# An S5 recurrence at every fourth time step in a two-layer fp32 transformer kernel

## The chip, the cores and the metric

One core of a Trainium2 chip runs the whole program. The metric is the device time of one execution in microseconds (us), lower being better.

## The reference

A stack of two layers over 512 positions of width 1024, batch 1, all in fp32. Each layer is an FFN (SwiGLU, hidden width 2816), a mixer, cross attention over 256 memory rows, and a second FFN; RMS norms stand before each. The mixer of layer 0 is the one that is changed: it projects the normed stream into the inputs of a chunked gated linear attention (GLA) and into `u`, 512 channels for S5. S5 has 32 groups of 16 channels with 64 complex states each:

```python
mag = exp(min(lam_re, -1e-4) * dt);  ab = mag * exp(i * lam_im * dt)     # one complex number per state
bb = f * B                                       # f = (ab - 1) / lambda
x[t] = ab * x[t-1] + bb @ u[t]                   # the recurrence, 512 time steps
y[t] = Re(C) @ Re(x[t]) - Im(C) @ Im(x[t]) + D * u[t]
y = gelu(y);  y = y * sigmoid(y @ w_glu + b_glu)
```

32 groups of 64 states make 2048 states, or 16 state tiles of 128 partitions (two groups each). `y` is joined to the GLA output and projected back. The mixer of layer 1 is a sparse attention and plays no part here.

## The kernel before, in words

**Weights.** All weight matrices are one stream of 381 blocks of 128x1024. SyncE loads them by halves into two raw slots (L236 to L266). GpSimd splits each half (L271 to L285) into a high and a low part, with a wait for TensorE to have finished the same half of the block two earlier, then three instructions: a 128x1 gate (L279), a rounding copy (L280) and a subtraction (L284). So GpSimd is at most two blocks ahead of TensorE. TensorE multiplies with three fp32r matmuls for one product (`mm3`, L310 to L312); one block gives 24 of them with 512 columns (a `tile`, L327), or with 256 columns for the keys and values of the memory (`kv_tile`, L452).

**Order.** Every engine has its own program, written out by hand, and semaphores join them: FFN 0, norm 1, then the even mixer. In it four tiles of `u` are projected (L340, `project`), then nine more tiles (the low-rank input of the decay, and q, k, r of the GLA), four blocks of GLA values (`values`, L487), the two alpha matmuls (L513), five blocks of memory keys (blocks 83 to 87), the two blocks of the S5 gate (`glu`, L624), and the GLA itself (`gla`, L522), whose first lines put three more memory key blocks ahead of its transposes (L525, L530). VectorE evicts each projected tile with `tile_out` (L1399).

**S5 before.** The recurrence is made real by rotating the states: with tables of cos and sin of the state's angle at each time, VectorE turns the input backwards, runs a real scan with factor `mag`, and turns the result forwards. The 16 tables of 128x1024 (cos, sin) are made during FFN 0: VectorE reduces the angle (`turns`, L1492, six instructions for each table), ScalarE takes the sines (`table`, L889) and writes the table to DRAM (L905); L1060 loads it again. At the end of FFN 0 VectorE multiplies C by f (`s5_output_matrices`, L1587, seven instructions). The loop of `s5` then goes over 16 state tiles, one at a time: TensorE makes the input (`inputs`, L592: K = 32 channels, 512 columns, one matmul for the real and one for the imaginary part), VectorE does four products from PSUM (L1638 to L1643), two sums, two scans of 512 steps (L1650, L1652), four products and two sums (L1655 to L1665), and TensorE multiplies by C (`outputs`, L605: 32 output channels, K = 128). Between them TensorE runs one weight block for each state tile (`ev_fill`, L773), in a fixed order: block, `inputs(j + 1)`, `outputs(j)`.

An fp32 matmul stands as two records in the trace, so that 32 calls of L602 give 64 records; an fp32 transpose is one record.

The lines that the text names, besides those: L324 is the mean square of a norm, L1309 its reciprocal, L1371 the low part of a hidden tile for the down projection (`part`), which TensorE needs before it takes that block, L1595 to L1602 the weight products, L1622 the sum with D * u, L1266 the low part of `y` that `glu` waits for, L1075 the gelu, L1088 the eviction of the values, L518 alpha, L1471 and L1472 two of the 16-column constants of S5, L741 transposes of the cross attention, L557 scores of the GLA, and L664 the logits of layer 1's indexer, whose calls go to partitions 0 to 63 and 64 to 127 in turn (L661).

## Time and profile before

| | us |
|---|---|
| median of 3 runs | 2435.99 |
| lowest, highest | 2433.85, 2439.0 |
| span of the profiled execution | 2432.6 |
| TensorE busy in it | 2301.4 |
| VectorE busy in it | 1154.7 |
| GpSimd busy in it | 1738.1 |

The profiled execution's span counts from its first to its last instruction. PE is TensorE's matmuls, PEld its weight loads, DVE VectorE, ACT ScalarE, POOL GpSimd. Durations of neighbours overlap a little, so the cost of one instruction in a row of them is read from the distance between starts. PEclk is the granted TensorE clock, 1.0 being 2.4 GHz and 0.5 being 1.2 GHz.

### The profile page before, as it was taken

The page shows a single profiled execution, that of the slowest core. Times are in us where ns is not written, and L with a number is a line of the kernel's source. Part 1 is how long each engine was busy: PE and PEld are TensorE (multiplying, and loading weights), DVE is VectorE, ACT ScalarE, POOL GpSimd, SP SyncE. Part 2 cuts the span into 40 slices and gives each one's busy share as a digit, 9 for nine tenths or more (in the row PEclk, how much of TensorE's full clock was granted, in tenths as well). Part 3 has the DMA queues.
Part 4 walks back from the last instruction along what each step waited for, and adds up shares of the span by engine and source line. Part 5 has one row for each costly group of instructions (what it writes and reads, how often), then busy time and mean ns, then how long its engine had stood idle before and what let it go on. Part 6 is the DMA issues. An engine that isn't in the chain of part 4 may idle for free.

```text
span 2432.6 us, 31471 instructions
## 1 busy us (share of the span) xinstructions
PE 2301.4 (95%) x10068; PEld 1820.2 (75%) x10068; DVE 1154.7 (47%) x1468; ACT 435.1 (18%) x752; POOL 1738.1 (71%) x2287
## 2 busy tenths in 40 slices
PE   7999999888789999999999999999987999999997
PEld 6888786445678688888778888877765777888886
DVE  7577717998644342224244223144598333322314
ACT  2122212002221221111122101120134222111011
POOL 7788877565648377878787788876764746777874
PEclk9999999897889999999999999999999999999998
DMA  4244334222212123333232323332221212323332
GB/s 158 90 144 146 126 95 134 78 91 78 70 57 95 49 83 95 98 96 100 91 108 87 99 95 95 100 94 83 78 74 53 81 58 77 96 95 97 96 96 82
DMA packets 117312, 226.02 MB, mean 93 GB/s; under 512 B 13040, under 2 KB 13312, under 8 KB 116864
## 3 DMA queue, kind: packets, MB, share of 16 engines
q1 hardware_dynamic: 110736, 203.61, 26.5%
q10 hardware_dynamic: 6512, 21.52, 2.6%
q8 instruction: 45, 0.74, 0.1%
q14 instruction: 19, 0.16, 0.0%
HBM read 214.59 MB, written 10.49 MB: 93 GB/s over the span
## 4 chain that ended last, share of the span: by engine, by line
PE 79%; DVE 15%; issue 2%; ACT 2%; POOL 1%; DMA 0%; SPq 0%; ACTq 0%; DVEq 0%; POOLq 0%
PE ps L310 24%; PE ps L311 24%; PE ps L312 24%; DVE tg L1286 1%; DVE arena L1738 1%; PE ps L728 1%; DVE col L1737 1%; PE ps L753 1%; DVE x L1276 1%; DVE sg L1652 1%; PE ps L602 1%; DVE sg L1650 1%; PE ps L643 1%; PE ps L613 1%; DVE arena L1757 0%
## 5 line engine op out<-in xcount | busy, mean ns | idle before, releaser
L310 PE MATMUL ps<-x,w_split 128*128 128x512 f32 (+1 forms) x2872 | 1126.3, 392 | 39.6 <-POOL w_split L284 17.4
L311 PE MATMUL ps<-x,w_split 128*128 128x512 f32 (+1 forms) x2872 | 1110.3, 387 | 0.0
L312 PE MATMUL ps<-x,w_split 128*128 128x512 f32 (+1 forms) x2872 | 1110.0, 386 | 0.0
L284 POOL TENSOR_TENSOR w_split<-w_raw,w_split 128x512 fp32r<-128x512 f32 x762 | 1021.5, 1341 | 63.5
L279 POOL TENSOR_TENSOR gate<-gate 128x1 f32<-128x1 f32 x758 | 257.7, 340 | 602.2 <-PE ps L312 601.9
L310 PEld LDWEIGHTS ps<-x,w_split 128*128 128x128 f32 x2872 | 544.4, 190 | 180.6 <-POOL w_split L284 28.0
L311 PEld LDWEIGHTS ps<-x,w_split 128*128 128x128 f32 x2872 | 544.5, 190 | 110.1 <-issue 4.8
L312 PEld LDWEIGHTS ps<-x,w_split 128*128 128x128 f32 x2872 | 543.9, 189 | 108.8
L280 POOL TENSOR_SCALAR w_split<-w_raw 128x512 fp32r<-128x512 f32 x762 | 509.4, 669 | 4.5 <-DMA w_raw<-in_stream 4.5
L1371 DVE TENSOR_TENSOR x<-arena,x 128x512 fp32r<-128x512 f32 x88 | 87.3, 1008 | 284.6 <-ACT x L941 284.6
L1328 DVE TENSOR_TENSOR tu<-ps,rstd 128x512 f32<-128x512 f32 x88 | 60.7, 689 | 319.5 <-PE ps L312 319.5
L887 ACT ACTIVATE sg<-tg 128x512 f32<-128x512 f32 x88 | 55.6, 632 | 652.1 <-DVE tg L1325 646.9
L1325 DVE TENSOR_TENSOR tg<-ps,rstd 128x512 f32<-128x512 f32 x88 | 60.6, 689 | 192.1 <-PE ps L312 191.3
L1334 DVE TENSOR_TENSOR arena<-sg,tu 128x512 f32 (+1 forms) x88 | 107.6, 1222 | 27.3 <-ACT sg L887 17.8
L1301 DVE SCALAR_TENSOR_TENSOR h<-ps,h 128x512 f32<-128x512 f32 x64 | 44.0, 688 | 142.9 <-PE ps L312 142.4
L941 ACT ACTIVATE x<-arena 128x512 fp32r (+1 forms) x88 | 53.7, 628 | 313.1 <-PE ps L312 312.4
L849 ACT ACTIVATE x<-h,vec 128x512 fp32r<-128x512 f32 x64 | 46.2, 722 | 210.7 <-DVE h L1301 206.9
L1399 DVE TENSOR_TENSOR arena<-ps,rstd 128x512 f32<-128x512 f32 x45 | 30.7, 689 | 101.4 <-PE ps L312 100.9
L1276 DVE SCALAR_TENSOR_TENSOR x<-h,vec,x 128x512 fp32r<-128x512 f32 x64 | 67.9, 1060 | 7.9 <-ACT x L849 7.9
L1286 DVE TENSOR_TENSOR tg<-tg,sq 128x512 f32<-128x512 f32 x63 | 70.0, 1110 | 0.1
L310 PE MATMUL ps<-w_split,x 128*128 128x256 f32 (+1 forms) x192 | 66.4, 346 | 1.3 <-POOL w_split L284 1.2
L311 PE MATMUL ps<-w_split,x 128*128 128x256 f32 (+1 forms) x192 | 61.1, 318 | 0.0
(234 smaller groups left out, 1576.5 us busy)
## 6 DMA issues: line engine op xcount, KB each, us to landing
w_raw<-in_stream SPq DMA_DIRECT2D x762, 256.0 KB, 2.6
s_tables<-kv ACTq DMA_DIRECT2D x16, 512.0 KB, 3.4
arena<-s_tables ACTq DMA_DIRECT2D x16, 512.0 KB, 3.3
out<-h ACTq DMA_DIRECT2D x8, 256.0 KB, 2.2
h<-in_xT SPq DMA_DIRECT2D x1, 1536.0 KB, 8.7
arena<-in_memT SPq DMA_DIRECT2D x1, 1024.0 KB, 10.5
arena<-in_memT ACTq DMA_DIRECT2D x1, 1024.0 KB, 4.8
h<-in_xT SPq DMA_DIRECT2D x1, 512.0 KB, 3.9
```

Source lines behind the costliest of these rows:

```text
L279: pool.tensor_tensor(gate[:, 0:1], gate[:, 1:2], gate[:, 1:2], ALU.add)
L280: pool.tensor_scalar(W[:, s, 0, c], raw[:, s, c], 1.0, 0.0, ALU.mult, ALU.add).then_inc(S(f"w_hi{'ab'[half]}"), 1)
L284: pool.tensor_tensor(W[:, s, 1, c], raw[:, s, c], W[:, s, 0, c].bitcast(F32), ALU.subtract).then_inc(split_ready if half else S("half_spli ...
L310: pe.matmul(dst, wh, xh, start=start, stop=False)
L311: pe.matmul(dst, wh, xl, start=False, stop=False)
L312: return pe.matmul(dst, wl, xh, start=False, stop=stop)
L1276: dve.scalar_tensor_tensor(X[to][:, k, 1, :], h[:, k, :], gain(n, k), X[to][:, k, 0, :].bitcast(F32), ALU.mult, ALU.subtract).then_inc(S(" ...
L1286: ins = dve.tensor_tensor(tg[:, 0, :], tg[:, 0, :], sq[:, k % 2, :], ALU.add)
L1325: dve.tensor_tensor(tg[:, s, :], ps[:, BANKS[2 * s], :], rstd[:], ALU.mult).then_inc(S("gate_ready"), 1)
L1328: dve.tensor_tensor(tu[:, s, :], ps[:, BANKS[2 * s + 1], :], rstd[:], ALU.mult).then_inc(S("up_ready"), 1)
L1334: dve.tensor_tensor(dst, sg[:, s:s + 1, :], tu[:, s:s + 1, :], ALU.mult).then_inc(S("hid_done"), 1)
L1371: dve.tensor_tensor(X[xo][:, ch:ch + 1, 1, :], hid[:, d, :], X[xo][:, ch:ch + 1, 0, :].bitcast(F32), ALU.subtract).then_inc(S("x_lo"), 1)
```

## The change

The recurrence is run for every fourth time step only. `u` is stored by offset within four steps (`by_offset`): four stretches of 128 columns. The input of step k of the strided recurrence is the sum over the four offsets of `ab^(3-s) * B` times `u`, so that `inputs` accumulates four matmuls of 128 columns; the tables and the scans have 128 steps, and one VectorE operand holds four state tiles side by side. The output at offset 3 is C times the state; at offsets 0 to 2 it is C times `ab^1` to `ab^3` times the state of the step before, plus a direct product of `u` with short taps (`C * f * ab^m * B`, block-diagonal, three 128x128 matrices for each of four channel tiles). 16 tables become 4. The powers of `ab` (32 more 16-column instructions), four sets of output weights and three sets of input weights are computed on VectorE, the latter between the parts of FFN 0's down projection; the input weights are turned by 24 transposes on TensorE beside the first `u` tiles, with copies by ScalarE, and the taps are 24 fp32 matmuls of 128x128x128, masked by VectorE. The order of TensorE's work in the stage is written out anew (`even_inputs`), and `y` goes to the other operand buffer. The masks of the taps, the eviction banks (`EV_BANKS` = 2, 3, 0 in turn) and the bank of the outputs (1) are new. `s5_input_weights` is like `s5_output_weights`, for powers of `ab` times B. The diff, cut to its core:

```diff
+STRIDE = 4
+NK = T // STRIDE
...
+                if beside is not None:
+                    beside(0)
                 mean_square(n)
                 for t in (2, 3):
                     tile(at + t, ((at + t) % 2, BANKS[t]), x)
+                    if beside is not None:
+                        beside(t - 1)
...
+            def s5_weights(i):
+                pe.wait_ge(S("h_ready"), 8)
+                pe.wait_ge(S("s5_mul"), 14)
+                if i == 0:
+                    pe.wait_ge(S("mat_in"), 16)
+                else:
+                    pe.wait_ge(S("s5_w"), 2 * i)
+                for c in range(2):
+                    for q in range(4):
+                        m = pe.transpose(ps[:, 6 + c, q * P:(q + 1) * P], b_in(i, c)[:, q * P:(q + 1) * P], ident)
+            def s5_taps(i):
+                if i == 0:
+                    pe.wait_ge(S("b_raw"), 16)
+                if i == 1:
+                    pe.wait_ge(S("std_ready"), 2)
+                if i == 2:
+                    pe.wait_ge(S("s5_tau"), 1)
+                for q in range(4):
+                    qc = slice(q * P, (q + 1) * P)
                     for c in range(2):
+                        m = pe.matmul(ps[:, TAP_BANKS[i], qc], area(A_BRAW + c * T)[:, qc], c_out(i, c)[:, qc],
+                                      start=(c == 0), stop=(c == 1))
+                m.then_inc(S("s5_tap_mm"), 1)
+            def s5_beside(step):
+                s5_weights(step)
+                if step == 2:
+                    s5_taps(0)
+            def s5_inputs(q):
+                pe.wait_ge(S("proj_out"), 4)
+                if q == 0:
+                    pe.wait_ge(S("s5b_in"), 16)
+                    pe.wait_ge(S("s5_tau"), 3)
+                    pe.wait_ge(S("rcol_ready"), 1)
+                    pe.wait_ge(S("s5_w"), 6)
+                else:
+                    pe.wait_ge(S("s5_read"), q)
+                for c in range(2):
+                    for s in range(STRIDE):
+                        for jj in range(4):
+                            r = slice(32 * jj, 32 * jj + 32)
+                            m = pe.matmul(ps[:, IN_BANKS[jj], c * NK:(c + 1) * NK], b_in(s, c)[r, q * P:(q + 1) * P],
+                                          Pt[q][r, s * NK:(s + 1) * NK], start=(s == 0), stop=(s == STRIDE - 1))
+                m.then_inc(S("s5_in_mm"), 1)
+            def s5_outputs(q):
+                pe.wait_ge(*((S("s5_y"), q) if q else (S("s5_tau"), 3)))
+                for i in range(3):
+                    pe.matmul(ps[:, OUT_BANK, i * NK:3 * NK], taps[:, i, q, :], Pt[q][:, 0:(3 - i) * NK],
+                              start=(i == 0), stop=False, skip_group_check=True)
+                pe.wait_ge(S("s5_x"), 2 * q + 2)
+                for r in (3, 0, 1, 2):
+                    for c in range(2):
+                        for jj in range(4):
+                            x = sq[:, c, jj * NK:(jj + 1) * NK]
+                            at = r * NK
+                            w = c_out((r + 1) % 4, c)[:, (4 * q + jj) * 32:(4 * q + jj + 1) * 32]
+                            out_r = ps[32 * jj:32 * jj + 32, OUT_BANK, :]
+                            if r == 3:
+                                m = pe.matmul(out_r[:, at:at + NK], w, x, start=False, stop=False,
+                                              skip_group_check=True)
+                            else:
+                                m = pe.matmul(out_r[:, at + 1:at + NK], w, x[:, 0:NK - 1], start=False,
+                                              stop=(r == 2 and c == 1), skip_group_check=True)
+                m.then_inc(S("s5_out_mm"), 1)
...
+                free = 1 if t == 4 else t - 2
+                tile(EV_AT + t, ((EV_AT + t) % 2, EV_BANKS[(t - 4) % 3]), 1, (S("proj_out"), free))
...
+                ev_tile(4)
+                s5_taps(1)
+                s5_taps(2)
+                rstd_columns(0)
+                ev_tile(5)
+                s5_inputs(0)
+                ev_tile(6)
+                s5_inputs(1)
+                ev_tile(7)
+                ev_tile(8)
+                s5_outputs(0)
+                ev_tile(9)
+                s5_inputs(2)
+                ev_tile(10)
+                s5_outputs(1)
+                ev_tile(11)
+                ev_tile(12)
+                s5_inputs(3)
+                s5_outputs(2)
+                pe.wait_ge(S("proj_out"), 13)
+                pe.wait_ge(S("s5_read"), 4)
+                values(EV_V_AT, 0, T, EV_V_BANKS)
+                values(EV_V_AT, 1, T, EV_V_BANKS)
+                s5_outputs(3)
+                values(EV_V_AT, 2, T, EV_V_BANKS)
+                values(EV_V_AT, 3, T, EV_V_BANKS)
+                gla_alpha()
+                for t in range(EARLY_KEYS):
+                    kv_tile(0, t, KV_BANKS)
...
+                    [(S("h_ready"), 3)], [(S("h_ready"), 8)], beside=s5_beside)
+            even_inputs()
...
+                    act.dma_start(area(A_CRAW, 2 * T), s5c.rearrange("p c j o -> p (c j o)")).then_inc(S("s5c_in"), 16)
+                    act.dma_start(area(A_BRAW, 2 * T), s5bt.rearrange("p c j o -> p (c j o)")).then_inc(S("b_raw"), 16)
+                    for i in range(last):
+                        if 4 <= i < 8:
+                            table(i - 4)
...
+            def s5_load(q):
+                act.dma_start(area(A_ROT + (q % 2) * 2 * T, 2 * T), s5_tables[q]).then_inc(S(f"s5_tab{q % 2}"), 16)
...
+                    act.wait_ge(S(f"tab_out{s}"), 32)
+                act.wait_ge(S("x_lo"), X_LO_HID[0] + FC)
+                act.dma_start(area(A_BIN[3], 2 * T), s5b.rearrange("p c q s -> p (c q s)")).then_inc(S("s5b_in"), 16)
+                act.dma_start(block_mask, blocks).then_inc(S("blocks_in"), 16)
+                for q in range(2):
+                    s5_load(q)
+            def s5_weights():
+                for i in range(3):
+                    act.wait_ge(S("s5_tr"), i + 1)
+                    for c in range(2):
+                        act.activation(b_in(i, c), ps[:, 6 + c, :], ACT.Copy).then_inc(S("s5_w"), 1)
...
+                act.wait_ge(S("s5_in_mm"), 4)
+                act.dma_start(chunk_mask, rows[1:2, :].to_broadcast([P, T])).then_inc(S("cmask_in"), 16)
+                act.dma_start(wal, w_alpha).then_inc(S("wal_in"), 16)
+                s5_gelu(2)
...
+                act.wait_ge(S("s5_out_mm"), 4)
+                act.wait_ge(S("block_done"), EV_V_AT + 4)
+                act.wait_ge(S("rcol_ready"), 1)
+                for tt in range(4):
+                    act.activation(val[:, tt, :], ps[:, EV_V_BANKS[tt], :], ACT.Copy,
+                                   scale=col[:, 16 + tt:17 + tt]).then_inc(S("gla_v"), 1)
+                gla_log()
...
+                        if i < 4:
                             next(parts)
+                        elif i < 8:
+                            turns(i - 4)
...
-                if f == 0:
-                    for s in range(2):
-                        turns(last, s)
+                    for d in range(4, 20):
+                        part(slice(d, d + 1), d % 4, base + d + 1)
+                        if 5 <= d < 9:
+                            s5_output_weights(d - 5)
+                        elif 9 <= d < 12:
+                            s5_input_weights(d - 9)
...
+            def ev_out(t):
+                if t < 4:
+                    dve.tensor_tensor(by_offset(Pt[t]), ps[:, BANKS[t], :].rearrange("p (k s) -> p k s", s=STRIDE),
+                                      rstd[:].rearrange("p (k s) -> p k s", s=STRIDE), ALU.mult
+                                      ).then_inc(S("proj_out"), 1)
...
                 chain(dve.tensor_tensor(fi, fi, den, ALU.mult))
                 yield
...
+                times(L_POW + 2, L_POW, L_POW)
+                times(L_POW + 4, L_POW + 2, L_POW)
+                for m in range(1, STRIDE):
+                    times(G_POW + 2 * m, G_POW, L_POW + 2 * (m - 1))
...
-                    ph, pl = sc5[:, C_PH + j:C_PH + j + 1], sc5[:, C_PL + j:C_PL + j + 1]
+                time = area(A_TIME).rearrange("p (j k) -> p j k", j=4)
+                ph = sc5[:, C_PH + 4 * q:C_PH + 4 * q + 4].unsqueeze(2).to_broadcast([P, 4, NK])
...
+                chain(dve.tensor_tensor(a, time, ph, ALU.mult))
+                chain(dve.tensor_scalar(b, a, MAGIC, MAGIC, ALU.add, ALU.subtract))
+                chain(dve.tensor_tensor(a, a, b, ALU.subtract))
+                chain(dve.tensor_tensor(b, time, pl, ALU.mult))
+                chain(dve.tensor_tensor(a, a, b, ALU.add))
+                chain(dve.tensor_scalar(b, a, MAGIC, MAGIC, ALU.add, ALU.subtract))
+                dve.tensor_tensor(a, a, b, ALU.subtract).then_inc(S("s5_turn"), 1)
...
+            def s5_output_weights(m):
...
+                dve.tensor_tensor(er, cr, gr, ALU.mult)
+                chain(dve.tensor_tensor(tA, ci, gi, ALU.mult))
+                dve.tensor_tensor(ei, cr, gi, ALU.mult)
+                chain(dve.tensor_tensor(tB, ci, gr, ALU.mult))
+                dve.tensor_tensor(er, er, tA, ALU.subtract).then_inc(S("s5_mul"), 1)
+                dve.scalar_tensor_tensor(ei, ei, -1.0, tB, ALU.mult, ALU.subtract).then_inc(S("s5_mul"), 1)
...
+            def s5_input_weights(i):
...
+            def s5_tap(i):
+                dve.tensor_tensor(taps[:, i], ps[:, TAP_BANKS[i], :].rearrange("p (q n) -> p q n", q=4),
+                                  block_mask.unsqueeze(1).to_broadcast([P, 4, P]), ALU.mult).then_inc(S("s5_tau"), 1)
...
+                for q in range(4):
...
+                    dve.wait_ge(S(f"s5_tab{q % 2}"), 16 * (q // 2 + 1))
+                    dve.wait_ge(S("s5_in_mm"), q + 1)
+                    if q >= 1:
+                        dve.wait_ge(S("s5_x"), 2 * q)
+                    op(dve.tensor_tensor(four(p1), vr, four(c), ALU.mult))
+                    n2 = op(dve.tensor_tensor(four(p2), vi, four(s), ALU.mult))
+                    op(dve.tensor_tensor(four(p3), vi, four(c), ALU.mult))
+                    dve.tensor_tensor(four(p4), vr, four(s), ALU.mult).then_inc(S("s5_read"), 1)
...
+                    ev_out(5 + 2 * q)
+                    for z, p, n in ((zr, p1, nr), (zi, p3, ni)):
+                        after(n)
+                        for jj in range(4):
+                            k = slice(jj * NK, (jj + 1) * NK)
+                            mag = sc5[:, C_MAG + 4 * q + jj:C_MAG + 4 * q + jj + 1].to_broadcast([P, NK])
+                            n = op(dve.tensor_tensor_scan(z[:, k], mag, p[:, k], 0.0, ALU.mult, ALU.add))
+                    ev_out(6 + 2 * q)
+                    after(n)
...
+                    if q >= 1:
+                        dve.wait_ge(S("s5_out_mm"), q)
                     after(n2)
+                    dve.tensor_tensor(xr, p1, p2, ALU.subtract).then_inc(S("s5_x"), 1)
                     after(n4)
-                    dve.tensor_tensor(xi, p3, p4, ALU.add).then_inc(S("s5_xi"), 1)
-                    if j % 4 == 0 and j >= 4:
-                        out(j // 4 - 1)
+                    dve.tensor_tensor(xi, p3, p4, ALU.add).then_inc(S("s5_x"), 1)
+                    if q >= 1:
+                        out(q - 1)
+                    if q >= 2:
+                        lower(q - 2)
+                out(3)
+                lower(2)
+                lower(3)
...
+                    x = X[0][:, 4 + n, :, :].rearrange("p c (k s) -> p c k s", s=STRIDE)
+                    lo_of(x[:, 1], by_offset(Pt[n]), x[:, 0], X_LO_GLU + n + 1)
...
+                ev_out(t)
+            dve.wait_ge(S("blocks_in"), 16)
+            s5_tap(0)
+            s5_tap(1)
+            s5_tap(2)
             rstd_columns(0)
+            ev_out(4)
+            s5()
```

## Rows read from the trace of the kernel before

**Rows 1.** the profile page: engine busy times, then 40 slices in tenths.

```profile
PE 2301.4 (95%) x10068; PEld 1820.2 (75%) x10068; DVE 1154.7 (47%) x1468; ACT 435.1 (18%) x752; POOL 1738.1 (71%) x2287
...
PEclk9999999897889999999999999999999999999998
```

**Rows 2.** busy time by stretch; the first line names the columns.

```profile
core 0: us, PE busy (x) PEld busy (x) DVE busy (x) ACT busy (x) POOL busy (x), PEclk, DMA share, GB/s
64.00:266.00 202.00, 201.73 (x880) 164.54 (x880) 144.53 (x176) 46.19 (x71) 167.93 (x213) 1.00 0.40 128
...
416.00:620.00 204.00, 171.32 (x570) 96.18 (x569) 191.71 (x242) 17.11 (x25) 120.02 (x109) 0.87 0.26 81
620.00:647.00 27.00, 21.02 (x112) 19.05 (x113) 18.44 (x20) 12.51 (x18) 22.71 (x27) 0.87 0.26 79
1325.00:1565.00 240.00, 240.00 (x1061) 198.87 (x1060) 65.23 (x74) 30.70 (x46) 192.00 (x265) 1.00 0.31 97
```

**Rows 3.** timeline of VectorE over one state tile, 428 to 440 us (start, duration).

```profile
428.04 0.68 DVE L1638 TENSOR_TENSOR tg<-ps,arena 128x512 f32<-128x512 f32 x1
...
431.63 1.22 DVE L1650 TENSOR_TENSOR_SCAN sg<-sc,tg 128x512 f32<-128x512 f32 x1
432.76 1.20 DVE L1652 TENSOR_TENSOR_SCAN sg<-sc,tu 128x512 f32<-128x512 f32 x1
...
439.22 0.69 DVE L1638 TENSOR_TENSOR tg<-ps,arena 128x512 f32<-128x512 f32 x1 [1.06 <-issue]
```

**Rows 4.** VectorE by line in 416:616 (count, busy us, mean ns, idle before).

```profile
L1652 DVE TENSOR_TENSOR_SCAN sg<-sc,tu 128x512 f32<-128x512 f32 x16 | 24.7, 1545 | 0.0
...
L1658 DVE TENSOR_TENSOR tu<-sg,arena 128x512 f32<-128x512 f32 x16 | 16.7, 1042 | 0.0
```

**Rows 5.** chain of waits, 612 to 648 us (start, us, what).

```profile
613.86 3.41 DVE x L1266 x3
...
620.04 0.50 PE ps L310
...
628.01 1.85 POOL w_split L284
...
647.03 1.07 PE ps L530 x5
```

**Rows 6.** input and output matmuls by source line (ns min, median, max).

```profile
L602 PE MATMUL ps<-arena,kv x64: 587/588/692, 414.5 to 596.8; 32*128 32x512 f32 x64
...
L613 PE MATMUL ps<-arena,kv x32: 592/617/1062, 427.7 to 614.3; 128*32 128x512 f32 x32
```

**Rows 7.** constants of S5 on VectorE in 86:93.

```profile
L1471 DVE TENSOR_TENSOR tiny<-tiny 128x16 f32<-128x16 f32 x1 | 1.1, 1146 | 0.0
...
L1472 DVE TENSOR_TENSOR tiny<-vec 128x16 f32<-128x16 f32 x1 | 0.2, 176 | 0.0
```

**Rows 8.** end of the first FFN: weight products on VectorE, a TensorE wait.

```profile
288.65 0.50 PE L310 MATMUL ps<-x,w_split 128*128 128x512 f32 x1 [0.97 <-DVE x L1371]
...
369.18 0.70 DVE L1595 TENSOR_TENSOR tu<-kv,sc 128x512 f32<-128x512 f32 x1 [1.85 <-DMA kv<-in_s5c]
...
375.27 1.39 DVE L1602 TENSOR_SCALAR kv<-kv 128x512 f32<-128x512 f32 x1
```

**Rows 9.** VectorE, the eviction of the fourth projected tile.

```profile
413.59 0.69 DVE L1399 TENSOR_TENSOR arena<-ps,rstd 128x512 f32<-128x512 f32 x1 [4.76 <-PE ps L312]
```

**Rows 10.** short fp32 matmuls and transposes on TensorE, three timelines.

```profile
1747.11 1.13 PE L664 MATMUL ps<-arena 64*128 64x256 f32 x8 [1.48 <-DVE arena L1875]
...
670.13 1.05 PE L557 MATMUL ps<-arena 64*128 64x128 f32 x8
...
826.04 1.07 PE L741 MATMUL ps<-mat,arena 128*128 128x128 f32 x8 [2.81 <-DVE arena L1818]
```

**Rows 11.** value copies and alpha matmuls, by source line (ns).

```profile
L1088 ACT ACTIVATE arena<-ps,col x4: 670/682/694, 574.2 to 576.0; 128x512 f32<-128x512 f32 x4
...
L518 PE MATMUL ps<-arena,kv x4: 1056/1057/1187, 576.8 to 579.5; 16*128 16x512 f32 x4
```

More of the change, by code:

```diff
@@ L133 @@
 NV = 141
-C_MAG, C_PH, C_PL, C_FR, C_FI = [16 * i for i in range(5)]
+C_MAG, C_PH, C_PL = [16 * i for i in range(3)]
+L_POW, G_POW = 0, 6
 A_TIME = FC * T
@@ L161, with build_trunk @@
 A_XPT = A_XP + 4 * T
-def build_trunk(nc, xT, memT, pos, vecs, w_alpha, s5b, s5c, mats, mask, rows, stream, out):
+def build_trunk(nc, xT, memT, pos, vecs, w_alpha, s5b, s5bt, s5c, blocks, mats, mask, rows, stream, out):
     with ExitStack() as ctx:
@@ L822, in _ @@
             for q in range(2):
[L823 removed]
+                values(OD_V_AT, q, 2 * P, BANKS)
             indexer_weights()
@@ L914, in ffn @@
                             s5_constants()
-                        if i == 3:
-                            for s in range(2):
-                                table(i, s)
-                    with act.Fori(4, last) as i:
-                        for s in range(2):
-                            silu(i, s)
-                        for s in range(2):
-                            table(i, s)
+                        if 4 <= i < 8:
+                            table(i - 4)
                 elif f == 2:
@@ L948, in ffn @@
                     silu(last, s)
-                if f == 0:
-                    for s in range(2):
-                        table(last, s)
                 act.wait_ge(S("hid_done"), FC * (f + 1))
@@ L1339, in ffn @@
                     parts = s5_constants()
-                    for i in range(4):
+                    for i in range(last):
                         for s in range(2):
@@ L1344, in ffn @@
                             memory(0)
-                        if i < 3:
+                        if i < 4:
                             next(parts)
-                        else:
-                            for s in range(2):
-                                turns(i, s)
-                    with dve.Fori(4, last) as i:
-                        for s in range(2):
-                            gate(i, s)
-                        for s in range(2):
-                            turns(i, s)
+                        elif i < 8:
+                            turns(i - 4)
                 elif f == 2:
@@ L1381, in ffn @@
                     gate(last, s)
-                if f == 0:
-                    for s in range(2):
-                        turns(last, s)
                 dve.wait_ge(S("hid_done"), FC * (f + 1))
@@ L1387, in ffn @@
                     beside()
-                with dve.Fori(1, 5) as i:
-                    for s in range(4):
-                        part(bass.ds(i * 4 + s, 1), s, i * 4 + (base + s + 1))
+                if f == 0:
+                    for d in range(4, 20):
[4 more added lines that the diff above has]
+                            s5_input_weights(d - 9)
+                else:
+                    with dve.Fori(1, 5) as i:
+                        for s in range(4):
+                            part(bass.ds(i * 4 + s, 1), s, i * 4 + (base + s + 1))
                 for d in (20, 21):
@@ new lines, in turns, with by_group, power @@
+                chain(dve.tensor_tensor(a, a, b, ALU.subtract))
[3 more added lines that the diff above has]
+                dve.tensor_tensor(a, a, b, ALU.subtract).then_inc(S("s5_turn"), 1)
+            def by_group(x):
+                return x.rearrange("p (j o) -> p j o", j=16)
+            def power(at):
+                return (powers[:, at + c, :].unsqueeze(2).to_broadcast([P, 16, 32]) for c in range(2))
@@ L1974, in lay_out @@
     s5b = np.zeros((P, 2, 4, P), f)
-    s5c = np.zeros((P, 2, S5_TILES, 32), f)
+    s5c, s5bt = (np.zeros((P, 2, S5_TILES, 32), f) for _ in range(2))
     for g in range(32):
```

321 lines of the change are left out of this document (126 added, 195 removed).

## The prediction

> **What bounds the kernel now.** First the page: TensorE is busy for 2301.4 of 2432.6 us, and its clock is full in nearly every slice [rows 1]. So the general answer is "TensorE", and a change to VectorE's work should be worth nothing. The table by stretch says where that is wrong. In an FFN (1325 to 1565) TensorE is busy without a break, 1061 records in 240.0 us, and 24 of them, one weight block, take 5.43 us. In the S5 stretch, 416 to 620, it is VectorE that is full: 191.7 of 204 us, with TensorE at 171.3 and at a mean clock of 0.87 [rows 2].
>
> One state tile on VectorE shows why. The four products from PSUM start 0.60 us apart, the two scans 1.13 us apart, and the next tile's first product comes 11.2 us after this one's [rows 3]. That is the quiet case; with GpSimd working beside it a product of two SBUF operands has a mean of 1.04 us and the second scan 1.55 us, not 0.60 and 1.13 [rows 4]. 16 tiles from 416 to 613.9 us [rows 5] are 12.3 us each. TensorE has less to do for a tile: a block (5.43), an input pair and an output pair, 1.7 us each at full clock (four records of 512 columns at 0.11 us for each 128 [rows 10]). It waits for VectorE, loses its clock, and then costs VectorE something in turn.
>
> What follows is the second half of the story. `glu` waits for the last low part of `y` until 620.0, and from there the chain runs through GpSimd's splits to the GLA transposes at 647.0 [rows 5]. GpSimd needs six instructions for a block: from the busy times and counts that is 4.35 us in the FFN, 4.73 where VectorE is busy for 72% of the time, 5.05 in 620 to 647, and 6.61 in the S5 stretch [rows 2]. A memory key block costs TensorE only about 2.8 us (24 matmuls of 256 columns), so a run of them goes at GpSimd's pace.
>
> **The change, part by part.** I count on the old clock from 413.5, where the fourth `u` tile is done (evicted at 413.6 [rows 9]), to the transposes of L530 at 647.0: 233.5 us.
>
> *Tables and powers.* 16 tables of six VectorE instructions become four of seven. TensorE runs 64 to 266 us without a break (201.7 of 202.0 [rows 2]), so this is worth nothing: what hides it is the weight stream. The 32 new 16-column instructions cost between 0.18 and 1.15 us each [rows 7]; with the durations seen that is some 10 us in one turn of the loop, where the turns before took longer in the same place. Nothing. The last two tables stood ahead of the down projection, and TensorE waited 0.97 us for a hidden tile there [rows 8]: -1.0. The two 512 KB loads at the start have 100 us to land, and the s5b and table loads, now behind VectorE's last hidden part, have 45 us.
>
> *Weights between the down parts.* Seven sets of six instructions. The old set of seven ran from 369.2 to 376.7, 1.07 us each [rows 8], so one set takes 6.4 us and, with the part, VectorE needs 7.3 us for a block of 5.43. A part is ready three blocks ahead of its use, 16 us; seven sets eat 13 us of that. VectorE should just get through. GpSimd is the doubt: beside a full VectorE it takes up to 6.6 us a block against TensorE's 5.43, over eight blocks 0 to +9 us. I take +3.0, nearer to the stretch with VectorE at 72%.
>
> *Transposes and first taps.* Eight transposes take 1.07 us [rows 10], of which the last record's tail overlaps: 3 x 1.0. Eight matmuls 128x128x128: four calls of 128 columns stand as 8 records in 1.05 us [rows 10], tail included, so 0.22 a call: 1.8. TensorE goes on with block 4 at 413.5 + 4.8 = 418.3. The six copies by ScalarE run behind the next `u` tile each time.
>
> *Inputs.* For each group 32 calls of 128 columns with K = 32, in four different groups of 32 rows in turn. Alone they are 32 x 0.22 = 7.0 us (before: eight calls of 512, 6.9). But the trace has calls that do not run alone: the indexer's go to rows 0 to 63 and 64 to 127 in turn, and eight records of 256 columns take 1.13 us [rows 10], the time of eight with 128. So two run at once. Four at once would be 1.75 us. I take two, 3.5 us, the nearest row.
>
> *Outputs.* Three tap matmuls, 768 columns: 1.3 us. 32 calls with 32 output columns, four column groups in turn: no row shows such calls together, L613 has one group at a time [rows 6]. Between 7.0 and 1.75; I take 3.5, as for the rows: 4.8 us.
>
> *VectorE.* A group of four tiles is now 16 instructions of 512 columns (12 of the recurrence, two evictions, the sum with D * u, a low part) and 8 scans of 128 (a quarter of 1.13 us and a fixed part, some 0.33 each): 12 us quiet, 16 with the durations of [rows 4]. TensorE has 28 us of work for a group. From `inputs(q)` to the finished state are 11 to 14 us, and TensorE has 19.8, over 25, 24.6 and 15.7 us of other work before it needs it. One wait stays: `values` needs the 13th eviction, which stands behind the scans of the last group, 7.5 to 9.5 us after `inputs(3)`, while TensorE arrives after `outputs(2)`, 4.8 us: 3.0.
>
> *The sum.* From 418.3: nine blocks 48.9, taps and the rstd transposes 4.0, inputs 4 x 3.5 = 14.0, outputs 4 x 4.8 = 19.2, values 21.7, the wait 3.0, together 110.8: the values are done at 529.1. Alpha waits for four copies of 0.68 [rows 11], 2.7, and takes 1.7 at full clock: 533.5. From the middle of the first key block (+1.4) eight more blocks come at GpSimd's pace: 4.9 us, between 4.35 and 5.05 [rows 2], as VectorE does the decay meanwhile: 39.2, and a last half, 1.4. The transposes start at 575.5: 71.5 us earlier. ScalarE's gates are done some 10 us before. With -1.0 and +3.0 in the FFN, 69.5. The strided evictions, and the eight strided splits of `y` ahead of the output projection, have no row; between nothing and twice 0.6 us they are 0 to +5, and I take 0, as they have the length of [rows 3]. 2432.6 - 69.5 = 2363.1 is the span; the median stands 3.4 above the profiled span, so 2366.5.
>
> A rule of the Trainium skill speaks against the change: TensorEngine Tiling (Array Packing), section Tiling Modes, says that a change of the tiling mode drains the array. With a record's tail of 0.16 us for each of 16 changes the time would be 2369; no run here shows it yet.
>
> **The rivals.**
> *A, four at once.* Inputs 1.75 and outputs 3.05 us. For it: the indexer's pairs overlap fully, so the row groups do not disturb each other [rows 10]. Against it: no row shows more than two, or any column groups. 4 x 3.5 less: 2352.5. The same skill page, section Theoretical Speedup, gives up to four times for a dimension of 32 or less.
> *B, one after the other.* A fixed cost for each weight load and matmul sets the pace: nowhere in [rows 10] do records come more than one each 0.11 us on average, whatever their columns. Then 7.0 and 8.3 us: +28, 2394.5.
> *C, GpSimd late in the down projection.* VectorE's products against its splits, at the S5 stretch's 6.6 us [rows 2]: +9 in place of +3, and some more where the parts come late: 2376.
> *D, slower.* The groups do not only fail to overlap, they break the pipeline: each record of 128 columns pays its share and its whole tail, 0.11 + 0.16 = 0.27 us (a 588 ns record of L602 [rows 6] less 0.43). 64 records are 17.3 us, 4 x 27.6 = 110 more: 2477. It decides from 0.19 us a record on (69.5 us over 512 records above the 0.055 assumed). The indexer's row is against it for the inputs; nothing is for the outputs, which alone would give 2422.
>
> That the change doesn't do what it says I leave out: loops, tables and instruction counts are in the diff.
>
> **How the numbers follow.** Forecast 0.45, A 0.20, B 0.20, C 0.10, D 0.05. The forecast's own range, with GpSimd at 4.35 to 5.5 us and the FFN at 0 to 9, is 2358 to 2378. A with the low bounds reaches 2345, B with the high ones 2403. I give 2343 to 2402, which leaves out D and the outer ends of A and B. A measurement of this kernel tells 0.2%, 4.9 us, from no change. All cases but D are faster by far more; of D I put 0.01 into no change.
>
> **What the profile would show.** VectorE's busy share in the S5 stretch falls from 0.94 to about a half; TensorE has no wait for VectorE but one near 3 us ahead of the values; `inputs` spans 3.5 us and `outputs` 4.8; the transposes of L530 start near 577 us (575.5 and the 2 of the FFN); the clock stays at 2.4 GHz from 416 to the values. I would be wrong if `inputs` took 7 us or more, if TensorE waited for GpSimd in the down projection for more than 9 us, or if waits for VectorE filled the time that the scans gave free.

## The result, and the profile after

The changed kernel takes 2365.68 us (median of 4 runs, 2365.23 to 2368.07) against 2437.38 for the kernel before on the same chip: ratio 0.972, 95% interval 0.9699 to 0.9741. The profiled span fell from 2432.6 to 2363.4 us. I had 2366.5.

In the changed kernel L338 to L340 are the three matmuls of a product, L670 is the input call, L678 the tap matmuls, L689 and L692 the output calls, L646 the taps, L550 alpha and L562 the GLA transposes, all on TensorE. On VectorE L1448 makes the low part of a hidden tile, L1642 to L1663 are the weight products, L1486 evicts a projected tile, L1779 to L1805 are the recurrence. On ScalarE L1179 copies the values and L1073 evicts a key tile. On GpSimd L307 is the gate, L308 the rounding copy and L312 the subtraction.

The page, to be laid beside [rows 1]:

```profile
span 2363.4 us, 31958 instructions
...
PE 2251.5 (95%) x10548; PEld 1827.9 (77%) x10548; DVE 1024.3 (43%) x1327; ACT 416.4 (18%) x721; POOL 1707.6 (72%) x2287
...
PEclk9999999998899999999999999999999999999998
```

Busy times by stretch, in the columns of [rows 2]. First the down projection with the weight products; then 416 to the last value matmul; then from there to the GLA transposes:

```profile
284.00:336.00 52.00, 45.46 (x194) 35.71 (x193) 51.59 (x43) 5.05 (x8) 49.32 (x51) 1.00 0.27 86
416.00:523.00 107.00, 102.15 (x911) 84.42 (x909) 58.92 (x102) 7.43 (x11) 59.57 (x82) 0.98 0.24 78
523.00:581.00 58.00, 45.47 (x248) 39.81 (x248) 20.21 (x20) 22.82 (x34) 46.59 (x58) 0.85 0.28 89
```

The S5 stretch is TensorE's now: it is busy for 102.2 of 107 us, at a clock of 0.98; VectorE went from 191.7 of 204 us [rows 2] to 58.9 of 107, a share of 0.55. The stretch behind it is GpSimd's. The down projection is where VectorE is full, 51.6 of 52 us. What TensorE waited for, first in the down projection, then from 410 to 590:

```profile
PE ps L338 <- POOL w_split L312: 3.9, 4, 1.2
PE ps L338 <- DVE x L1448: 2.6, 2, 1.6
...
PE ps L338 <- POOL w_split L312: 10.5, 7, 3.4
PE ps L338 <- DVE arena L1486: 4.2, 1, 4.2
PE ps L550 <- ACT arena L1179: 2.7, 1, 2.7
```

The first input step and the first output step on TensorE:

```profile
433.79 0.39 PE L340 MATMUL ps<-x,w_split 128*128 128x512 f32 x1
434.11 2.07 PE L670 MATMUL ps<-arena 32*128 32x128 f32 x64
436.11 0.50 PE L338 MATMUL ps<-x,w_split 128*128 128x512 f32 x1
436.44 0.40 PE L339 MATMUL ps<-x,w_split 128*128 128x512 f32 x1
...
455.71 1.46 PE L678 MATMUL ps<-arena 128*128 128x384 f32 x6
457.10 0.65 PE L689 MATMUL ps<-sq,kv 128*32 128x128 f32 x16
457.56 1.48 PE L692 MATMUL ps<-sq,kv 128*32 128x127 f32 x48
458.97 0.50 PE L338 MATMUL ps<-x,w_split 128*128 128x512 f32 x1
```

An input step is 2.0 us from its start to the next block's, not the 3.5 I took; an output step 3.3, not 4.8. The starts of single records in the trace come four within 20 ns and then 91 ns later: four groups at once, 112 ns for a record of each.

A change of the shape has a price too. The block's first record starts 0.20 us after the last record of an input or output step. Behind the taps, which use the whole array, it starts 0.03 us after the last of them:

```profile
417.27 1.95 PE L646 MATMUL ps<-kv,arena 128*128 128x128 f32 x16
418.98 0.48 PE L338 MATMUL ps<-x,w_split 128*128 128x512 f32 x1
419.30 0.40 PE L339 MATMUL ps<-x,w_split 128*128 128x512 f32 x1
```

From the last short record to the block's second it is 0.54 us in the one case and 0.35 in the other, so a change costs 0.19 us; ahead of an input step it is again 0.19, ahead of an output step's short calls 0.12. About half of this lies inside the 2.0 and 3.3 us. (The 0.3 us between the block's first two records are no sign of it: they stand behind the taps as well.)

VectorE's part of a group, beside [rows 3]:

```profile
436.31 0.69 DVE L1779 TENSOR_TENSOR tg<-ps,arena 128x512 f32<-128x512 f32 x1 [6.54 <-PE ps L670]
...
440.52 2.41 DVE L1793 TENSOR_TENSOR_SCAN sg<-sc,tg 128x128 f32<-128x128 f32 x4
442.85 1.34 DVE L1793 TENSOR_TENSOR_SCAN sg<-sc,tu 128x128 f32<-128x128 f32 x4
444.11 0.66 DVE L1486 TENSOR_TENSOR arena<-ps,rstd 128x512 f32<-128x512 f32 x1
...
447.70 0.68 DVE L1805 TENSOR_TENSOR sq<-tu 128x512 f32<-128x512 f32 x1
```

12.1 us for four state tiles (with two evictions), where one took 11.2. The first group has no sum with D * u yet; the others take 15.3, 12.7 and 11.7 us with it; the 15.3 are the group that ran longest beside GpSimd's splits.

### The profile page after: what moved, and what is told of

Same layout as the page of the kernel before. It is cut to its first block, busy times and chain, and to the rows that moved or that the text cites. A ratio compares the mean times of both kernels' runs of the same rounds, so it can differ in the third digit from the quotient of the medians.

```text
span 2363.4 us, 31958 instructions
## 1 busy us (share of the span) xinstructions
PE 2251.5 (95%) x10548; PEld 1827.9 (77%) x10548; DVE 1024.3 (43%) x1327; ACT 416.4 (18%) x721; POOL 1707.6 (72%) x2287
## 4 chain that ended last, share of the span: by engine, by line
PE 77%; DVE 12%; issue 5%; POOL 4%; ACT 1%; DMA 0%; POOLq 0%; SPq 0%; DVEq 0%; ACTq 0%
PE ps L338 24%; PE ps L340 24%; PE ps L339 24%; POOL w_split L312 2%; POOL w_split L308 2%; DVE tg L1369 2%; PE ps L800 1%; DVE arena L1879 1%; DVE col L1878 1%; PE ps L825 1%; DVE x L1359 1%; POOL gate L307 1%; DVE arena L1898 0%; DVE col L1901 0%; DMA h<-in_xT 0%
## 5 line engine op out<-in xcount | busy, mean ns | idle before, releaser
L338 PE MATMUL ps<-x,w_split 128*128 128x512 f32 (+1 forms) x2872 | 1125.5, 392 | 43.8 <-POOL w_split L312 25.3
L340 PE MATMUL ps<-x,w_split 128*128 128x512 f32 (+1 forms) x2872 | 1110.0, 386 | 0.0
L312 POOL TENSOR_TENSOR w_split<-w_raw,w_split 128x512 fp32r<-128x512 f32 x762 | 1015.8, 1333 | 63.6
L338 PEld LDWEIGHTS ps<-x,w_split 128*128 128x128 f32 x2872 | 545.0, 190 | 171.5 <-POOL w_split L312 31.7
L307 POOL TENSOR_TENSOR gate<-gate 128x1 f32<-128x1 f32 x758 | 243.5, 321 | 563.8 <-PE ps L340 561.0
L340 PEld LDWEIGHTS ps<-x,w_split 128*128 128x128 f32 x2872 | 544.7, 190 | 108.5
L308 POOL TENSOR_SCALAR w_split<-w_raw 128x512 fp32r<-128x512 f32 x762 | 500.2, 656 | 4.3 <-DMA w_raw<-in_stream 4.3
L1448 DVE TENSOR_TENSOR x<-arena,x 128x512 fp32r<-128x512 f32 x88 | 87.7, 1013 | 246.0 <-ACT x L1028 246.0
L338 PE MATMUL ps<-w_split,x 128*128 128x256 f32 (+1 forms) x192 | 65.5, 341 | 5.1 <-DVE arena L1486 4.2
L1492 DVE TENSOR_TENSOR arena<-ps,rstd 128x512 f32<-128x512 f32 x32 | 21.9, 691 | 96.5 <-PE ps L340 96.2
```

Of the source, the lines that this page charges most:

```text
L307: pool.tensor_tensor(gate[:, 0:1], gate[:, 1:2], gate[:, 1:2], ALU.add)
L308: pool.tensor_scalar(W[:, s, 0, c], raw[:, s, c], 1.0, 0.0, ALU.mult, ALU.add).then_inc(S(f"w_hi{'ab'[half]}"), 1)
L312: pool.tensor_tensor(W[:, s, 1, c], raw[:, s, c], W[:, s, 0, c].bitcast(F32), ALU.subtract).then_inc(split_ready if half else S("half_spli ...
L338: pe.matmul(dst, wh, xh, start=start, stop=False)
L340: return pe.matmul(dst, wl, xh, start=False, stop=stop)
L1448: dve.tensor_tensor(X[xo][:, ch:ch + 1, 1, :], hid[:, d, :], X[xo][:, ch:ch + 1, 0, :].bitcast(F32), ALU.subtract).then_inc(S("x_lo"), 1)
```

## The experiments

### Do the calls overlap because their groups come in turn?

Three kernels that change nothing but the order of the calls: e1 and e2 in the input step, e3 in the output step.

```
e1   for c in range(2):
-        for s in range(STRIDE):
-            for jj in range(4):
+        for jj in range(4):
+            for s in range(STRIDE):
e2   for c in range(2):
-        for s in range(STRIDE):
-            for jj in range(4):
+        for s, jj in [(s, 2 * h + j) for h in range(2) for s in range(STRIDE) for j in range(2)]:
e3 - for r in (3, 0, 1, 2):
-        for c in range(2):
-            for jj in range(4):
+    for jj in range(4):
+        for r in (3, 0, 1, 2):
+            for c in range(2):
```

> The changed kernel with the 32 calls of an input step in another order: all four time steps of one group of 32 rows, then the next group. Same calls, same number, same data. In the changed kernel 64 records of an input step take 2.07 us, 31 ns each. Theory T (the groups run at once because they come in turn): now each record waits for the one before, 0.11 us as the short calls in the kernel before, 7.0 us a step, 4 x 5.0 = 20 us more, 2385.7 us. Rival S (a call with K = 32 costs 31 ns whatever the order): 2.07 us a step, 2365.7 us.

> The changed kernel with the calls of an input step ordered so that two row groups come in turn, then the other two. Theory T: two at once, 0.055 us a record, 3.5 us a step (the price that the prediction took), 4 x 1.45 = 6 us more, 2371.5 us. If the floor of 31 ns is the issue of a record and two groups are enough to reach it: 2.1 us, 2365.7 us. Rival S: 2365.7 us too.

> The changed kernel with the 32 calls of an output step ordered by column group: all eight calls of one group of 32 output columns, then the next. In the changed kernel the 64 records take 1.9 us. Theory T: 0.11 us a record, 7.0 us a step, 4 x 5.1 = 20.5 us more, 2386 us. Rival S (32 columns make a call short whatever the order): 2365.7 us.

The first input step of e2:

```profile
434.82 2.84 PE L670 MATMUL ps<-arena 32*128 32x128 f32 x64
```

and of e1:

```profile
435.29 5.13 PE L670 MATMUL ps<-arena 32*128 32x128 f32 x64
```

The same 64 records take 2.07 us with four groups in turn, 2.84 with two, 5.13 with one. Rival S is out: shortness alone is not it. T is right in kind and too high in size, since where the order moves on to the next group, its first three records still start beside the last ones of the old group (2 to 7 ns apart in the starts), so even the serial order is not 7.0. Two in turn give 2.84 for the same reason and not 3.5. In time: e1 2381.08 us (ratio to before 0.976, 0.9743 to 0.9777), 15.4 above the changed kernel's median, where the four steps add 11.9 (the other three take 5.03 each). Part of the rest is the clock: in e1's trace TensorE, though busy without a break, fell to 1.2 GHz for 3.4 us at 440.1 and at 477.6 us, at the end of the first and the third serial step, which it did in no other version of the changed kernel between 416 and 490 us; e2 2368.11 (0.9721, 0.9702 to 0.974), where they add 3.1: not to be told from the changed kernel.

e3 took 2376.86 us (0.9743, 0.9724 to 0.9762). Its output calls run from 458.39 to 464.3 us, 5.9 in place of 1.9, so 16 us in all, and yet the kernel is only 11 slower. The wait in front of the values shows most of why: there TensorE had 4.2 us to spare, and the longer `outputs(2)` fills it. Nor does the clock fall there (see the section on the hardware), which is worth another 1.5.

```profile
PE ps L338 <- DVE arena L1486: 0.2, 1, 0.2
```

### How much of the gain is VectorE's?

b1 is the kernel before with the recurrence left out for three quarters of its columns:

```
-  op(dve.tensor_tensor(p1, vr, c, ALU.mult))
+  op(dve.tensor_tensor(p1[:, 0:128], vr[:, 0:128], c[:, 0:128], ALU.mult))
   (the other nine products and sums, and both scans, likewise; not xr and xi)
```

> The kernel before with VectorE's recurrence cut to a quarter: products from PSUM, sums, scans and back-rotations work on the first 128 of 512 columns, so the recurrence is left out for the rest; TensorE's calls and everything else stay. Theory V (VectorE's time in the S5 stretch is what the change took away): VectorE needs some 5.5 us a tile, TensorE 5.4 + 3.5 = 8.9; 13 tiles end near 532, five key blocks at GpSimd's pace, glu and the key blocks behind it: L530 near 592 to 597 in place of 647, so 50 to 55 us less, 2382 to 2387 us. Rival W (the shorter input and output calls are most of the gain, 16 x 3.4 us of TensorE's time become 21 us): not more than 20 us less, 2417 us or above.

2379.19 us, ratio 0.9758 (0.9742 to 0.9774), span 54.9 below that of before. Its busy times from 416 on and its chain where the GLA transposes begin (L530):

```profile
416.00:530.00 114.00, 114.00 (x389) 65.91 (x388) 60.89 (x186) 2.55 (x3) 50.85 (x74) 1.00 0.36 113
...
594.84 0.89 PE ps L530 x8
```

TensorE is full for 114 of 114 us at full clock, and the transposes start 52 us earlier than at 647.0 [rows 5]. Theory V holds: cutting VectorE's time alone gives 54.9 of the 69.2 us. The 14.3 left I put down to TensorE, from the traces; the other half of the test, the short calls with VectorE's time left as it was, was not run. In b1 a block with its input and output calls takes 9.4 us, so about 3.8 us of calls in each of the 13 tiles up to the end of the values, 49 us (those of the last three tiles lie beside GpSimd's splits). The changed kernel has 21 us of them, but 8 us of new transposes and taps and the wait of 4.2, and it comes into the stage 2.0 us later and loses 1.5 to the clock. That makes 12.3 us; its values end at 523.2 us, b1's at 535.1.

### Are the waits that are left worth their time?

```
e4 (down projection)
-  if 5 <= d < 9:
-      s5_output_weights(d - 5)
-  elif 9 <= d < 12:
-      s5_input_weights(d - 9)
+  if 5 <= d < 19:
+      next(weights)          # three of a set's six instructions
e5 (TensorE, behind the values; KV_BANKS = [5, 3])
+  kv_tile(0, 0, KV_BANKS)
   gla_alpha()
-  for t in range(EARLY_KEYS):
+  for t in range(1, EARLY_KEYS):
e6 (VectorE, last group)
+  if q == 3: ev_out(11); ev_out(12)     # ahead of the products
-  ev_out(5 + 2 * q)   ...   ev_out(6 + 2 * q)
+  if q < 3: ev_out(5 + 2 * q)   ...   if q < 3: ev_out(6 + 2 * q)
e7   the three together
```

> The changed kernel with the seven sets of weight products cut in halves of three instructions, one half behind each of 14 down parts in place of one set behind each of 7. In the changed kernel TensorE waits 6.5 us there: 3.9 for GpSimd's splits, whose block takes 6.0 us beside a VectorE that is full, and 2.6 for late parts, as a set takes 9.0 us. Theory P (both waits come from doing the sets faster than the parts are used): VectorE keeps pace (about 5.2 us a part), GpSimd falls behind by at most 0.2 us a block; waits of 0 to 3 us, 3.5 to 6.5 us less, 2359 to 2362 us. Rival Q (the contention for VectorE's and GpSimd's operands costs what it costs, spread or not): the waits show again over 14 parts, 2365.7 us.

> The changed kernel with the first memory key block ahead of the two alpha matmuls, and its PSUM bank exchanged with the second's so that it needs none of ScalarE's value copies. In the changed kernel GpSimd stands still for 8.1 us (523.6 to 531.8) with both weight buffers full, while TensorE waits 2.7 us for the copies and takes 2.9 for alpha. Theory G (GpSimd's pace sets the stretch from the values to the GLA transposes, so its idle time there is worth itself): it resumes 5.6 us earlier, all behind it comes 4.5 to 5.6 us earlier, 2360 to 2361 us. Rival K (the decay for the GLA, which stays where it is, or the key tiles' evictions by ScalarE end last): within 1 us of 2365.7.

> The changed kernel with the 12th and 13th evictions ahead of the last group's products on VectorE, in place of ahead of and behind its scans. In the changed kernel TensorE waits 4.2 us for the 13th before the values. Theory E: the wait falls to the read of the last input bank, 0.7 us; 3.5 us less, 2362.2 us. Rival F (the stretch behind is paced by GpSimd, and an earlier start of the values is lost in it): 2365.7 us.

> The changed kernel with the three edits together: half sets, the key block ahead of alpha, the evictions first. If the three are independent, as theories P, G and E have it: 5 + 5 + 3.5 = 13.5 us less, 2352 us. If they overlap (one wait taking the place of another), less than 9 us less, above 2357 us.

Medians 2361.38, 2362.97, 2363.84 and 2356.43 us; ratios to before 0.9708, 0.9715, 0.9717 and 0.9682 (0.9657 to 0.9707). They ran on another chip, where the kernel before takes 2430.86 us, so the ratios are the fair comparison. By them e4 to e6 gain 2.9, 1.2 and 0.7 us and e7 9.3, between its two expectations. The first three are each within the interval of 0.972, so for them the traces must speak.

e4: TensorE's waits in the down projection, 6.5 us before, are

```profile
PE ps L338 <- DVE x L1359: 2.2, 3, 1.3
PE ps L338 <- POOL w_split L312: 2.1, 7, 0.4
```

of which the first line is the norm behind the down projection, in every kernel. No wait for a part is left, and 4.1 us are won there (start of GpSimd's 41st and 141st split, each against the changed kernel's). Theory P.

e5: GpSimd resumes at 525.2 us, not 531.8, but then stands still again:

```profile
525.21 0.19 POOL L307 TENSOR_TENSOR gate<-gate 128x1 f32<-128x1 f32 x1 [1.15 <-PE ps L340]
...
537.91 0.73 POOL L307 TENSOR_TENSOR gate<-gate 128x1 f32<-128x1 f32 x1 [4.30 <-PE ps L340]
```

TensorE waits 3.4 us ahead of the third key block for ScalarE, which evicts the first key tile only behind the decay's log steps. The GLA transposes start at 577.0 us, 3.7 earlier: theory G, with part of its gain turned into the new wait. How much of it reaches the end, the 1.2 us by the ratio can't tell.

e6: the wait of 4.2 us for L1486 is not among the waits of its trace, and the splits behind the values come 3.2 us earlier, the transposes 2.9, both counted from the S5 stage's start: theory E. Its profiled run was longer than the changed kernel's all the same, by what the clock did elsewhere (below).

e7 joins the three. Against the changed kernel its transposes start at 566.37 in place of 580.68, 14.3 us earlier, and its end comes 7.9 us earlier. To separate this from scatter, it ran again beside the changed kernel, together with e8, which adds one move on ScalarE:

```
e8 (ScalarE, behind the value copies)
+  fill(0, KV_BANKS, 1)
   gla_log()
   ...
-  fill(0, KV_BANKS, EARLY_KEYS)
+  fill(0, KV_BANKS, EARLY_KEYS - 1)
```

> The changed kernel once more, unaltered, beside the two versions below on the same chip: 2365.7 us, within 0.2% (2361 to 2370).

> The version with the three edits again, now beside the changed kernel. Its transposes for the GLA started 14.3 us earlier than in the changed kernel's trace, its end came 7.9 us earlier. If the 14.3 are the edits' and the rest is the clock in the stages behind, which differs from one execution to the next: 7 to 14 us below the changed kernel of the same call, 2352 to 2359 us. If the edits bring nothing beyond the scatter of chips and calls: within 4 us of the changed kernel.

> The version with the three edits, and on ScalarE the eviction of the first key tile ahead of the three log steps of the decay. In the version before it TensorE waits 3.4 us for that eviction ahead of the third key block, and GpSimd stands still for 3.8 us at the same time. Theory G (GpSimd's idle time in this stretch is worth itself): 3.4 to 3.8 us less than the version with the three edits. Rival K (the decay, delayed by the eviction, or a later wait takes it back): the same, within 1 us.

The changed kernel: 2364.89 us, ratio 0.9718 (0.9692 to 0.9744). The three edits: 2353.81, 0.967 (0.9644 to 0.9696), 11.1 us or 0.5% better. The intervals of the two ratios just touch, but the slowest of its five runs, 2357.14, is below the fastest of the changed kernel's five, 2363.6. e8: 2352.05, 0.9662 (0.9637 to 0.9687); its wait for the eviction is gone,

```profile
PE ps L338 <- POOL w_split L312: 8.5, 5, 2.6
PE ps L338 <- ACT kv L1073: 0.5, 1, 0.5
```

but of the 3.4 to 3.8 us only a part shows: 2.7 in the trace at the transposes (counted from the S5 stage's start, against the second run of the three edits; 2.2 against the first) and 1.8 in the median. That is more than rival K allows and less than theory G has. It is the fastest of all, though not to be told from the three edits alone.

## Why the prediction was right, and where it was only lucky

**The mechanism held.** VectorE bounded the S5 stretch, and b1 shows that taking its time away is worth 54.9 us. A group takes it 11.7 to 15.3 us (12 to 16 said), its share is 0.55 (about a half), the one wait ahead of the values is 4.2 us (3.0). The clock stayed at 2.4 GHz from 416 to 495.9 us, the end of that wait; it fell there, just ahead of the values.

**The time is right to a microsecond by errors that cancel.** On the new clock, with the 2 us that I gave to the FFN:
- *Input and output steps.* "I take two, the nearest row" is the term that was mis-sized: four run at once, in rows and in columns, as rival A had it. The eight steps cost 21 us in place of 33. The indexer's row only showed two because its calls have only two groups. The Trainium skill, TensorEngine Tiling (Array Packing), section Theoretical Speedup, gives up to four times for a dimension of 32; by e1 and e3 the gain over the serial order is 2.5 times for rows (5.13 to 2.07 us) and 3 for columns (5.9 to 1.9); that order still overlaps a little, and against 64 records at 0.11 us, 7.0, it would be 3.4 and 3.6. Its rule that a change of the tiling mode drains the array (Tiling Modes) agrees with the 0.20 us between the last record of a step and the block behind it, against 0.03 behind the taps. At 0.12 to 0.19 us the 16 changes come to some 2.8 us, half of it in the steps' own time; I had priced it at 2.5, and left it out of the sum.
- *The values* ended at 523.2, not 531.1 (529.1 and 2): 12.1 us less in the steps and 1.3 at the start of the stretch, against 1.2 more of waiting for the eviction, 0.6 for a split, 1.6 in the blocks beside other calls (5.54 to 5.68 us in place of 5.43), and 1.5 that the values lost in a spell of 3.4 us at 1.2 GHz from 495.9 us. Had the rest held, the result would have been 2358.6, over halfway to rival A's 2352.5.
- *The stretch behind the values* took that back: 57.5 us to the transposes in place of 46.4. I had counted eight blocks after the first; the trace has nine (18 half splits, 531.8 to 579.1 us). GpSimd splits by pairs of blocks, the first halves of both and then the second halves, so one half of the second block was still to do and one of the eleventh stood ahead of the last that was needed. That is a miscount, 5.1 us. GpSimd's pace was 5.1 us a block, not 4.9 (1.5 us), it stood still for 1.7 us more with both buffers full beside `glu`, the first key block held its buffer for 3.1 us and not 1.4, and copies and alpha took 5.5 and not 4.4.
- *The FFN.* The old last tables cost more than the 0.97 us that I took: GpSimd's 101st split starts at 289.9 us, 3.9 earlier than before. (1.7 of the 3.9 are there by the 41st, and there the traces of the changed kernel and its variants differ among themselves by up to 2.3, so that part may be scatter.) Then the weight products take 5.9 back (its 121st split starts 2.0 later), not 3.0; this is rival C's mechanism at two thirds of its price, with a part of its own that I excluded: "VectorE should just get through". One set takes 9.0 us with its part, not 7.3, so the parts themselves came late, 2.6 us of the 6.5.
- *The GLA* gave 3.6 us: its transposes are 66.1 us earlier, what follows it 69.7. The change does nothing there, so this is luck: b1, which has the old GLA, keeps its distance to the changed kernel within 0.2 us over this stage, and a second trace of the changed kernel (c1) gains another 2.9 us in it.

So the transposes came at 580.7, 3.2 us behind my 577.5, and the GLA made that good. The table:

| step | forecast, new clock | measured |
|---|---|---|
| block 4 starts | 420.3 | 419.0 |
| values done | 531.1 | 523.2 |
| first key block | 535.5 | 528.7 |
| GLA transposes | 577.5 | 580.7 |
| span | 2363.1 | 2363.4 |

**Rivals.** B and D are out: no step costs 7 us, even in the serial order, and none 17. D's mechanism, each record paying its whole tail, is contradicted by 64 records in 2.07 us. A is right in the price of a step (1.75 and 3.05 said, 2.0 and 3.3 measured) and wrong in the time. C's mechanism is there at two thirds of its price.

## What to carry to other kernels

Short calls go in turn over the groups of rows or columns that they leave free: same calls, same number, a third to two fifths of the time of one group after another. When a bound is lifted, ask at once which buffer is full while the next stage's engine stands still: here 11 us were to be had from three moves of whole instructions, two of them found by TensorE's waits and one by the idle time of an engine (GpSimd) that is on the path only there. And a sum that comes out right needs its own check, term by term: mine had two errors of 11 to 12 us.

## What the runs showed of the hardware

**VectorE and GpSimd in lockstep.** Beside GpSimd's splits, VectorE's products of two SBUF operands do not slow evenly; they alternate (GpSimd's instructions of the same time stand behind them):

```profile
302.32 1.14 DVE L1644 TENSOR_TENSOR kv<-arena,powers 128x512 f32<-128x512 f32 x1
303.38 1.78 DVE L1645 TENSOR_TENSOR tu<-arena,powers 128x512 f32<-128x512 f32 x1
305.19 1.14 DVE L1646 TENSOR_TENSOR kv<-kv,tu 128x512 f32<-128x512 f32 x1
306.25 1.78 DVE L1647 SCALAR_TENSOR_TENSOR kv<-kv,tu 128x512 f32<-128x512 f32 x1
307.95 0.68 DVE L1448 TENSOR_TENSOR x<-arena,x 128x512 fp32r<-128x512 f32 x1
...
303.00 1.61 POOL L312 TENSOR_TENSOR w_split<-w_raw,w_split 128x512 fp32r<-128x512 f32 x1
305.18 0.62 POOL L308 TENSOR_SCALAR w_split<-w_raw 128x512 fp32r<-128x512 f32 x1
305.88 1.60 POOL L312 TENSOR_TENSOR w_split<-w_raw,w_split 128x512 fp32r<-128x512 f32 x1
```

They start 1.1 and 1.8 us apart by turns; quiet ones, such as L1784 and L1786 at 438.72 and 439.32 us, start 0.60 apart, so 0.5 and 1.2 us are waiting. By their times it is for a split to end: L1645 ends 0.55 us after the split that ends at 304.61, and L1647 0.55 us after the one that ends at 307.48, near the 0.60 of a quiet product. GpSimd in turn needs 5.8 us a block (49.32 us for 51 of its instructions, six a block) and not 4.35. This agrees with the Trainium skill, SBUF — State Buffer, section SBUF: two separate sides, which has the two engines share a port pair that one holds for a whole instruction. Products with one operand in PSUM keep their 0.60 us beside the splits: from L1779 at 448.51 us to L1784 at 450.91 there are four of them, while GpSimd split a block from 448.4 on. Even a short scan waits: four scans of 128 columns took 2.41 us while a split ran (440.57 to 442.02 us) and 1.34 behind it.

**The clock falls behind a wait.** In the six traces that have the wait of 4.2 us ahead of the values (the changed kernel, c1, e1, e2, e4, e5), TensorE's clock fell to 1.2 GHz for 3.4 or 6.8 us within 1.1 us of the wait's end. In the five where the wait is gone (e3, e6, both runs of e7, e8) it stayed full from 416 to 523 us. The changed kernel and e6:

```profile
485.00:507.00 22.00, 17.78 (x183) 14.44 (x182) 12.28 (x24) 1.27 (x2) 8.44 (x13) 0.92 0.19 64
...
485.00:507.00 22.00, 20.63 (x201) 16.64 (x200) 14.22 (x23) 1.26 (x2) 14.07 (x18) 1.00 0.26 83
```

So such a wait costs more than its length, here 4.2 and 1.5 us.

**The clock of one and the same stage differs between executions, by some 3 us.** The GLA ran at a mean clock of 0.81 before:

```profile
647.00:757.00 110.00, 97.88 (x485) 80.41 (x484) 46.74 (x64) 20.21 (x34) 56.72 (x79) 0.81 0.20 62
```

and at 0.86 in the changed kernel,

```profile
581.00:690.00 109.00, 98.00 (x495) 80.31 (x494) 49.33 (x65) 22.61 (x34) 60.81 (x85) 0.86 0.21 67
```

with the same matmuls; this goes with the 3.6 us of the section before (in b1, with the old GLA, it was 0.86 too). And in e3, e4, e5, e6 and the first run of e7 TensorE fell to 1.2 GHz for 6.8 us between 1905 and 1934 us, in a stage that no edit touches; the distance to the changed kernel's trace grew there by 3.0 us each time. In both traces of the changed kernel, e1, e2, e8 and the second run of e7 it did not, but e1, e2 and b1 had such a fall between 756 and 778 us, for 3.0 us as well. What decides it was not tried. It is why a gain of 3 to 5 us was read from the stage it was made in and not from the end.
